# First of four weight sums by a load and an adding transfer instead of by VectorE

## The reference

```python
proj = hn @ w_in                       # hn: 512 x 2048
...
g = jax.nn.sigmoid(gate_logits.reshape(b, s, N_BRANCHES, D_MODEL))
y = g[:, :, 0] * ua + g[:, :, 1] * ub + g[:, :, 2] * uc
return x + y @ w_out
```

## Time and profile before

| | |
|---|---|
| median of 3 runs | 2146.58 us (2145.89 to 2147.29) |
| span of the profiled execution, first to last instruction | 2144.3 us |
| TensorE busy | 2114.5 us, 99% |
| VectorE busy | 1638.5 us, 76% |
| ScalarE busy | 920.1 us, 43% |
| GpSimd busy | 76.9 us, 4% |
| share of the chain that ended last: TensorE, VectorE, ScalarE, transfers | 83%, 6%, 3%, 2% |
| mean granted TensorE clock | 1.000 of full |

### The profile page before, as it was taken

How to read it: one execution, slowest core, us unless ns; L and a number is a source line. 1 busy time by engine, 2 the same in 40 slices (tenths; PEclk the granted TensorE clock), 3 DMA queues, 4 the chain that set the end, 5 groups by cost and what they waited for, 6 DMA issues and landing times.

```text
span 2144.3 us, 35680 instructions
## 1 busy us (share of the span) xinstructions
PE 2114.5 (99%) x12168; PEld 1835.5 (86%) x12168; DVE 1638.5 (76%) x2684; ACT 920.1 (43%) x1581; POOL 76.9 (4%) x145
## 2 busy tenths in 40 slices
PE   7899999999999999999999999999999999999999
PEld 6788888788887999999998888888787888888999
DVE  6887877775667888888886666666868776777887
ACT  6434454433335444444444444444545444223433
POOL 0000000000000000000000000000000000010000
PEclk9999999999999999999999999999999999999999
DMA  9766432565544343343333222222222223665543
GB/s 381 266 243 234 178 96 97 208 219 191 177 144 132 123 144 128 121 142 131 119 105 119 89 88 88 88 90 87 70 81 78 89 89 121 205 213 181 193 142 109
DMA packets 85935, 310.76 MB, mean 145 GB/s; under 512 B 9765, under 2 KB 12213, under 8 KB 77505
## 3 DMA queue, kind: packets, MB, share of 16 engines
q1 hardware_dynamic: 71568, 258.24, 35.6%
q0 software_dynamic: 11520, 46.68, 6.2%
q10 hardware_dynamic: 2738, 4.47, 0.6%
HBM read 284.41 MB, written 24.94 MB: 144 GB/s over the span
## 4 chain that ended last, share of the span: by engine, by line
PE 83%; DVE 6%; ACT 3%; DVEq 3%; DMA 2%; issue 1%; ACTq 0%
PE bank L425 18%; PE bank L427 18%; PE bank L426 18%; PE bank L1172 9%; PE bank L1174 9%; PE bank L1173 9%; DVE w_lo L419 2%; ACT w_hi L409 1%; PE bank L554 1%; PE bank L585 1%; DMA w_raw<-stream 1%; DMA front_raw<-stream 1%; PE bank L567 1%; DVEq L414 1%; ACT probs L637 1%
## 5 line engine op out<-in xcount | busy, mean ns | idle before, releaser
L425 PE MATMUL bank<-x_hi,w_hi 128*128 128x512 f32 x2000 | 789.1, 395 | 3.6 <-ACTq L1357 1.2
L427 PE MATMUL bank<-x_hi,w_lo 128*128 128x512 f32 x2000 | 779.1, 390 | 0.0
L426 PE MATMUL bank<-x_lo,w_hi 128*128 128x512 f32 x2000 | 778.6, 389 | 0.0
L419 DVE TENSOR_TENSOR w_lo<-w_raw,w_hi 128x512 fp32r<-128x512 f32 x468 | 324.2, 693 | 315.6 <-ACT w_hi L409 286.6
L409 ACT ACTIVATE w_hi<-w_raw 128x512 fp32r<-128x512 f32 x468 | 295.9, 632 | 572.4 <-PE bank L427 477.0
L425 PEld LDWEIGHTS bank<-x_hi,w_hi 128*128 128x128 f32 x2000 | 375.4, 188 | 94.4 <-issue 8.9
L1172 PE MATMUL bank<-x_hi,pw_hi 128*128 128x256 f32 x1568 | 444.0, 283 | 0.8 <-issue 0.7
L1173 PE MATMUL bank<-x_lo,pw_hi 128*128 128x256 f32 x1568 | 443.7, 283 | 0.0
L1174 PE MATMUL bank<-x_hi,pw_lo 128*128 128x256 f32 x1568 | 443.7, 283 | 0.0
L427 PEld LDWEIGHTS bank<-x_hi,w_lo 128*128 128x128 f32 x2000 | 375.4, 188 | 79.6
L426 PEld LDWEIGHTS bank<-x_lo,w_hi 128*128 128x128 f32 x2000 | 375.7, 188 | 75.4 <-issue 0.2
(11 more groups left out here) (214 smaller groups left out, 1840.5 us busy)
## 6 DMA issues: line engine op xcount, KB each, us to landing
w_raw<-stream SPq DMA_DIRECT2D x234, 512.0 KB, 3.7
pw_raw<-stream SPq DMA_DIRECT2D x112, 512.0 KB, 4.6
wmod<-w_mod_rows SPq DMA_DIRECT2D x32, 1024.0 KB, 6.7
front_raw<-stream SPq DMA_DIRECT2D x16, 1024.0 KB, 9.0
wmod<-w_mod_rows POOLq DMA_DIRECT2D x16, 1024.0 KB, 5.2
sig_store<-logits POOLq DMA_DIRECT2D x45, 256.0 KB, 2.5
sig_back<-sig_store SPq DMA_DIRECT2D x8, 768.0 KB, 5.9
gate_sig<-sig_store SPq DMA_DIRECT2D x7, 768.0 KB, 5.8
```

The lines of the kernel that those rows point to most:

```text
L419: nc.vector.tensor_tensor(w_lo[:, q, :], raw_quarter(s), w_hi[:, q, :].bitcast(F32), ALU.subtract).then_inc(lo_ready, 1)
L425: nc.tensor.matmul(bank_ap[:, :tokens], hi, x_hi[:, kx, :], start=start, stop=False)
L426: nc.tensor.matmul(bank_ap[:, :tokens], hi, x_lo[:, kx, :], start=False, stop=False)
L427: return nc.tensor.matmul(bank_ap[:, :tokens], lo, x_hi[:, kx, :], start=False, stop=stop)
```

## The change

SyncE now loads a21 a second time, straight into `w_sum[0]` (`first_row_load`), and when that has landed GpSimd's queue issues a transfer of a22 from DRAM that adds to what lies there (`second_row_add`, `accum_op=ALU.add`). `first_sum_added` counts these, and it is what ScalarE's split of S1 and VectorE's S2 wait for. VectorE makes only S2, S3 and S4, so `w_sum_made` counts three for each pair. The load may only start when `w_sum[0]` is free: when the low part of S3 of the pair before is made (`pw_lo_ready`), or, for the first pair of a stage, when all the low parts of the input sums are (`t_ready` at 8 or 16). Two semaphores are saved elsewhere (`dist_loaded`, `urow_zeroed`).

```diff
+            def first_row_load(pair):
+
+                if pair.positive() and not (pair.i is None and pair.c == PAIRS):
+                    sp.wait_ge(pw_lo_ready, ((pair - 1).times(7) + 5).value())
+                else:
+                    sp.wait_ge(t_ready, pair.c // PAIRS * KT // 2 + KT // 2)
+                src = stream[(pair.times(2) + (PANELS + 1)).pick(), :, :8 * P]
+                sp.dma_start(w_sum[0][:, :], src.rearrange("a p n -> p (a n)")).then_inc(first_row_loaded, 16)
+
             def load_factor(l, i=None):
...
                 elif a == 0:
-                    sp.wait_ge(w_sum_made, ((pair - 2).times(4) + 4).value())
+                    sp.wait_ge(w_sum_made, ((pair - 2).times(3) + 3).value())
...
             for l in range(12):
                 load_factor(l)
+                if l == 5:
+                    first_row_load(At(0))
+                if l > 4 and l % 4 == 3:
+                    first_row_load(At(l // 4))
             with steps(sp, 1, PAIRS // 3) as i:
                 for l in range(12):
                     load_factor(l, i)
+                    if l % 4 == 3:
+                        first_row_load(At(l // 4, 3, i))
...
             for l in range(6):
                 load_factor(first + l)
+            first_row_load(At(PAIRS))
             sp.wait_ge(xp_stored, 16 * (KT - 2))
             for p in range(OUT_PAIRS):
                 back_load(2 + 2 * p)
                 for l in range(4 * p + 6, min(4 * p + 8, 4 * OUT_PAIRS)):
                     load_factor(first + l)
+                if p + 1 < OUT_PAIRS:
+                    first_row_load(At(PAIRS + p + 1))
...
-            act.wait_ge(urow_zeroed, 1)
+            act.wait_ge(shift_ready, 1)
...
-                    act.wait_ge(w_sum_made, (f.pair.times(4) + (f.o - 1)).value())
+                    if f.o == 2:
+                        act.wait_ge(first_sum_added, (f.pair + 1).times(16).value())
+                    else:
+                        act.wait_ge(w_sum_made, (f.pair.times(3) + (f.o - 2)).value())
...
-            mod_biases(KT, 4, 0.0).then_inc(shift_ready, 1)
             nc.vector.memset(urow[:, :PAD], 0.0)
             nc.vector.memset(urow[:, PAD + T:], 0.0)
-            dve.drain().then_inc(urow_zeroed, 1)
+            mod_biases(KT, 4, 0.0).then_inc(shift_ready, 1)
...
                 dve.drain()
-                if f.o == 2:
-                    for a in (2, 3):
-                        dve.wait_ge(raw_of(f, a)[1], raw_of(f, a)[2])
-                to, one, two, op = {2: (w_sum[0], a21, a22, ALU.add), 3: (w_sum[1], w_sum[0], a11, ALU.subtract),
+                if f.o == 3:
+                    dve.wait_ge(first_sum_added, (f.pair + 1).times(16).value())
+                if f.o == 5:
+                    dve.wait_ge(raw_of(f, 2)[1], raw_of(f, 2)[2])
+                to, one, two, op = {3: (w_sum[1], w_sum[0], a11, ALU.subtract),
...
-                if f.o in (0, 1, 2, 6) and f.ahead(3):
+                if f.o in (0, 1, 2):
                     weight_sum(f.ahead(3))
...
                 if s == 15:
-                    weight_sum(Factor(2))
                     factor_lo(Factor(1))
...
                     token_sums_lo(KT - 2)
-                    weight_sum(Factor(PRODUCTS + 2))
                     factor_lo(Factor(PRODUCTS + 1))
...
-            for b in range(3):
+            def second_row_add(pair):
+
+                pool.wait_ge(first_row_loaded, (pair + 1).times(16).value())
+                src = stream[(pair.times(2) + (PANELS + 1)).pick(), :, 8 * P:].rearrange("a p n -> p (a n)")
+                pool.dma_start(w_sum[0][:, :], src, accum_op=ALU.add).then_inc(first_sum_added, 16)
+
+            for b in range(2):
                 sigmoid_store(At(b), At(1), b, b % 2)
+            second_row_add(At(0))
+            sigmoid_store(At(2), At(1), 2, 0)
+            second_row_add(At(1))
...
+                sigmoid_store(At(3 + 2 * b, 6, i) if i else At(3 + 2 * b + 6 * n), At(2, 2, i) if i else At(2 + 2 * n), b, 0)
+                if i:
+                    second_row_add(At(b + 2, 3, i))
+                elif 3 * n + b + 2 < PAIRS:
+                    second_row_add(At(3 * n + b + 2))
+                sigmoid_store(At(4 + 2 * b, 6, i) if i else At(4 + 2 * b + 6 * n), At(3, 2, i) if i else At(3 + 2 * n), b, 1)
...
             pool.dma_start(x_store[KT - 1, :, :], x_prime[:, :]).then_inc(xp_stored, 16)
+            for p in range(OUT_PAIRS):
+                second_row_add(At(PAIRS + p))
```

More of the change, by code:

```diff
@@ L314, in program @@
         mem_loaded = [sem(f"mem_part{n}_loaded") for n in range(4)]
-        c_loaded, dist_loaded = sem("c_loaded"), sem("dist_loaded")
+        c_loaded = sem("c_loaded")
         x_loaded = [sem(f"x_part{n}_loaded") for n in range(4)]
@@ L336, in program @@
         mem_k_ready, mem_v_ready, mem_out_stored = sem("mem_k_ready"), sem("mem_v_ready"), [sem(f"mem_out{n}_stored") for n in range(2)]
-        urow_zeroed, urow_ready, urow_used = sem("urow_zeroed"), sem("urow_ready"), sem("urow_used")
+        urow_ready, urow_used = sem("urow_ready"), sem("urow_used")
         sig_ready, sig_used = sem("sig_ready"), sem("sig_used")
@@ L348, in program @@
         pw_loaded = [sem(f"pw_raw{n}_loaded") for n in range(6)]
+        first_row_loaded, first_sum_added = sem("first_row_of_sum_loaded"), sem("first_sum_added")
         w_sum_made, pw_hi_ready, pw_lo_ready = sem("w_sum_made"), sem("pw_hi_ready"), sem("pw_lo_ready")
@@ L775, in dve_window @@
                 if s == 1 and w.extra:
-                    dve.wait_ge(dist_loaded, 16)
+                    dve.wait_ge(cols_loaded, 32)
                     dve.wait_ge(c_stored, 16)
@@ L986, in load_factor @@
                 elif a == 2:
-                    sp.wait_ge(w_sum_made, ((pair - 1).times(4) + 4).value())
+                    sp.wait_ge(w_sum_made, ((pair - 1).times(3) + 3).value())
                 else:
-                    sp.wait_ge(w_sum_made, ((pair - 1).times(4) + 3).value())
+                    sp.wait_ge(w_sum_made, ((pair - 1).times(3) + 2).value())
                 src = stream[(pair.times(2) + (PANELS + a // 2)).pick(), :, a % 2 * 8 * P:(a % 2 + 1) * 8 * P]
@@ L1550, in _ @@
                 split_hi(act, At(4 * FIRST["b"] - 3 + t))
-            act.dma_start(dist_a[:, :], dist_in).then_inc(dist_loaded, 16)
+            act.dma_start(dist_a[:, :], dist_in).then_inc(cols_loaded, 16)
             for _ in range(COPIES - 1):
@@ L1967, in weight_sum @@
             def weight_sum(f):
-                a11, a12, a21, a22 = (raw_of(f, a)[0] for a in range(4))
+                a11, a12, a21 = (raw_of(f, a)[0] for a in range(3))
                 dve.drain()
-                if f.o == 2:
-                    for a in (2, 3):
-                        dve.wait_ge(raw_of(f, a)[1], raw_of(f, a)[2])
-                to, one, two, op = {2: (w_sum[0], a21, a22, ALU.add), 3: (w_sum[1], w_sum[0], a11, ALU.subtract),
+                if f.o == 3:
[3 more added lines that the diff above has]
+                to, one, two, op = {3: (w_sum[1], w_sum[0], a11, ALU.subtract),
                                     4: (w_sum[0], a12, w_sum[1], ALU.subtract), 5: (w_sum[1], a11, a21, ALU.subtract)}[f.o]
@@ L2298, in sigmoid_store, with pair_sigmoids @@
                                logits[slot][:, :]).then_inc(sig_stored[slot], 16)
-            for b in range(3):
+            def second_row_add(pair):
[3 more added lines that the diff above has]
+            for b in range(2):
                 sigmoid_store(At(b), At(1), b, b % 2)
+            second_row_add(At(0))
+            sigmoid_store(At(2), At(1), 2, 0)
+            second_row_add(At(1))
             pool.wait_ge(c_neg_ready, 1)
             pool.dma_start(c_store, f_a[:HEADS_B, :]).then_inc(c_stored, 16)
-            with steps(pool, 0, PAIRS // 3) as i:
+            def pair_sigmoids(b, i, n):
+                sigmoid_store(At(3 + 2 * b, 6, i) if i else At(3 + 2 * b + 6 * n), At(2, 2, i) if i else At(2 + 2 * n), b, 0)
[4 more added lines that the diff above has]
+                sigmoid_store(At(4 + 2 * b, 6, i) if i else At(4 + 2 * b + 6 * n), At(3, 2, i) if i else At(3 + 2 * n), b, 1)
+            with steps(pool, 0, PAIRS // 3 - 1) as i:
                 for b in range(3):
-                    for e in range(2):
-                        sigmoid_store(At(3 + 2 * b + e, 6, i), At(2 + e, 2, i), b, e)
+                    pair_sigmoids(b, i, None)
+            for b in range(3):
+                pair_sigmoids(b, None, PAIRS // 3 - 1)
             pool.wait_ge(c_stored, 16)
```

## The result

The changed kernel takes 2199.93 us (median of 4 runs, 2197.9 to 2202.19), the kernel before, beside it, 2146.23 us (2145.43 to 2147.29). The ratio is 1.025, with a 95% interval of 1.0235 to 1.0266: 2.5% slower, some 54 us, where 12.3 were forecast. The profiled execution has a span of 2196.3 us, 52.0 above that of before.

The account below looks back on a forecast made before the run. TensorE was taken as the bound; 2.5 + 8.3 + 1.5 = 12.3 us on the span of 2144.3 gave 2156.6 in a profile, 2158.9 us as the runs' median. Own range 2154.8 to 2160.6, 8-in-10 range 2153 to 2200.

Parts of the forecast that it names:

- What bounds the kernel: TensorE bounds it; VectorE's work in the pairs is hidden behind matmuls, so removing sums buys nothing inside a stage.
- The start of the first stage: TensorE's product 2 of the first paired stage waits for S1, at 711.1 instead of 708.6: loss 2.5 us.
- The start of the second stage: TensorE's product 2 waits for load and adding transfer, at 2013.7 instead of 2005.44: loss 8.3 us.
- The clock: Behind the second stage's first wait, matmuls run at half speed for a while: 1.5 us, bounds 0 and 2.2.
- The loop: In steady pairs, buffer free, load, add, split and VectorE's chain take 14.5 us + A, within a pair's 20.2.
- A: Time from GpSimd's issue to the landing of a22 added into w_sum[0]: taken as 5.2 us.
- the forecast's limit: In the steady pairs, the adding transfer may take at most 5.7 us for the turn to fit 20.2 us.
- the forecast's formula: In each later pair, TensorE waits for A - 5.7 us if A is over 5.7 us.
- The load's own term: In the steady pairs, the load of a21, third of a burst, takes 6.0 us.
- The first: Rival: A over 5.7 us, so TensorE waits in each of 26 later pairs; 2196 us at A = 7.0; chance 0.35.
- The second (not slower): Rival: the first S1 of each stage comes in time; gain up to 1.3 us, 2145.3 us; chance 0.05.
- The third: Rival: the clock does not fall, 2157.4 us, or the second start's load takes 6.5 us, 2161.5; no separate chance.

Follow-up runs that it names:

- the kernel with held blocks: Changed kernel with the load ahead of the pair's two blocks, and those blocks held until the adding transfer has landed: 2158.17 us.
- the copy: Changed kernel with GpSimd's transfer copying a22 over w_sum[0] instead of adding it: 2171.53 us; also with the load issued before the two blocks: 2178.93 us.
- the load ahead: Changed kernel with SyncE issuing the load of a21 into w_sum[0] before the pair's two blocks, not behind them: 2205.59 us.
- the kernel with S1's own buffer: Changed kernel with a separate buffer for S1, its load issued before the two blocks once S1's low part is made: 2162.74 us.

## Why the prediction was right or wrong

**What bounds the kernel: right.** VectorE's sums lie beside matmuls. With the loop closed and the starts given back, 26 of 28 sums gone leave 2147.42 us against 2146.48.

**The start of the first stage: right.** Forecast were the issue at 703.1, product 2 at 711.1 and a loss of 2.5 us. It was issued at 702.62, and TensorE's row is

```profile
710.62 0.39 PE L1191 MATMUL bank<-x_hi,pw_hi 128*128 128x256 f32 x1 [1.96 <-DVE pw_lo L1985]
```

a loss of 2.0 against the 708.6 of before. The transfer took 5.4 us.

**The start of the second stage: right.** Everything there is some 29 us later than before. The load took 4.0 us (3.9 forecast), the adding transfer 5.7, by GpSimd's and VectorE's rows:

```profile
2034.45 0.90 POOL L2323 DMA_DIRECT2D w_sum<-stream  x1 [29.59 <-DMA w_sum<-stream]
```

```profile
2040.22 1.23 DVE L1998 TENSOR_TENSOR w_sum<-w_sum,pw_raw 128x1024 f32<-128x1024 f32 x1 [10.05 <-DMA w_sum<-stream]
```

and TensorE's wait is 9.4 us, as forecast:

```profile
2033.17 0.28 PE L1193 MATMUL bank<-x_hi,pw_lo 128*128 128x256 f32 x1
2042.86 0.55 PE L1191 MATMUL bank<-x_hi,pw_hi 128*128 128x256 f32 x1 [9.42 <-issue]
```

Product 0 had begun at 2027.53, so product 2 came 15.3 us after it, and 7.0 before (1998.44 to 2005.44): a loss of 8.3, the forecast's number.

**The clock: too small for this kernel.** The forecast held 1.5 us, with bounds of 0 and 2.2, all behind the second start's wait. In the changed kernel half-speed matmuls cost 2.8 us there (0.21 us apart from 2042.86 to 2048.97, at a granted clock of 0.50), and 1.6 more behind the first start's wait (from 710.62 to 714.33, at 0.55), where none were forecast. That is 4.4 us, 3.9 more than before. In the kernel with held blocks, with nearly the same two waits (2.07 and 9.1 us), it is 2.1 us, 1.6 more than before: there the forecast's number came out, in part by luck. The length of the rest alone does not tell whether half speed follows. After 2.92 us of rest the matmuls from 840.95 on are 0.21 us apart, and so they are after 1.96 us at 710.62; in the kernel with held blocks, after 2.07 us, they are 0.12 apart again from the second on, and the granted clock is 1.00 from 710 to 714. The Trainium skill's "TensorE: Matmul & The Clock Gate" (part 1) has as a rule that the throttled state is the default and activity releases it. The traces agree with the second half of it: full speed comes back while matmuls run, at 714.33, 844.10 and 2048.97. In the whole changed kernel the half-speed matmuls cost 10.8 us more than before, but by the sum below most of that is no extra: in a pair whose turn is set by the loop, slower matmuls only use up time in which TensorE would have waited. No run here tries this apart.

**The loop: the frame was right, and its size A failed.** The text reads "Sum: 14.5 + A. It must be at most 20.2, so A at most 5.7." The failed step is "I take 5.2, the row with as many bytes read, since writes can go beside reads", used for the steady pairs: there the transfer took 6.9 us in the first paired stage and 8.2 in the second. The limit was a little too high as well. In the changed kernel all but the adding transfer comes to 14.75 us in the first stage and 14.7 in the second, which leaves 5.4 to 5.5 for A; the copy took the 5.7 of the forecast's limit, and its loop did not close. With the medians the forecast's formula gives 1.2 us in 20 pairs and 2.5 in 6, 39 us; with the 12.0 by which the span of the kernel with held blocks, where only the starts are left, is over that of before, it is 51, against the 52.0 measured. With the table's mean turns in place of the formula it would be 55, so a hit within a microsecond is in part luck.

The load's own term was right (6.0 forecast, 5.7 measured), though a row was misread for it: the 6.5 us of the earlier trace rows belong to the second load of that burst, issued at 811.88. The third, issued at 813.33, took 6.3.

**Why A was off.** At the starts, with no block load beside it, it is 5.4 and 5.7 us, 0.2 to 0.5 above the row that I took. The rest is the block loads in flight beside it: 5.6 us in the median with none (the kernel with held blocks), 6.9 with two (19 of the 21 transfers of the changed kernel's first stage) and 8.6 with four (the load ahead). The forecast had a load's time in a burst (6.5 against 3.9) and used it for the load, but priced the adding transfer, which goes beside the same blocks, by the median of a row, without asking what stood beside that row's transfers. The sixteen of 1024 KB in the earlier trace rows were not alone either, and not alike: ten took 5.0 to 5.4 us, with one or two block loads beside them for a part of that time, and the six others 5.7 to 9.2. That spread was the warning. The mean share of 0.38 of the engines' time, which I held against the rival, says nothing of the moment in which the transfers meet: from 811 to 823 us the share was 0.58 in the kernel before, and from 800 to 815 us it is 0.82 in the changed one. So the forecast had a margin of 0.5 us a pair on a term with an error of over one, and a chance of 0.58 on the wrong side of it.

The estimate by the Trainium skill's "Collectives: The Full Stack" (bandwidth ceiling: a reduction costs two source reads, not the add) and "DMA: Bandwidth & Descriptors" (anatomy of a transfer) was 4.4 us. The trace does not agree: it is 5.4 to 5.7 with no block load beside it. A copy of as many KB took 3.8 to 4.2 at the same places, and the addition made it 1.2 to 1.9 longer.

**The rivals.** The first is what happened. Its 2196 us are 4 below the runs: its pairs (26 times 1.3, 34 us) are 5 below the 39 of the medians, its starts (15.9) are 4 above the 12.0, and the rest is the microsecond that is missing above and the profiled run, which was 2 us below the runs' median. The second (not slower) has nothing for it: the first S1 was late at both starts. The third puts both its times into the forecast's own range, but 2161.5 lies above that range's 2160.6. **VectorE's busy time** went down by 35 us (34 forecast), and the store behind the adding transfer went out late without anything waiting for it for more than 3.4 us in total.

What stays open: how much of the 8.2 us of the second stage comes from x1's loads and the results' stores, which only that stage has. With the blocks held the transfer took 5.5 us there, with the results' stores beside it; x1's loads stand behind the blocks in SyncE's queue and were held with them. In the last pair of the stage no block load is beside it, but x1's loads and the results' stores are: it took 7.2 us in the changed kernel (at 2168.63) and 5.7 where VectorE makes the first S1. So they can cost something without any block, and not always.

## What to carry to other kernels

Work taken off an engine that is not the bound buys nothing, but the transfers that replace it form a loop with the buffer they fill, and its length, not their bandwidth, has to stay under the period. Price each transfer of such a loop in the company that it will have there, beside the burst that is released at the same moment, and not by the median of a row of its kind; look at that row's single transfers and at what stood beside them. A margin of 0.5 us on a sum of 20 is no margin. Two ways closed the loop here: a buffer that comes free earlier, or holding back the transfers that nobody waits for until the one that is waited for has landed; and at the start of a stage, where nothing runs ahead, the old engine is best kept.

## What the runs showed of the hardware

- GpSimd's adding transfer of 512 KB took 5.4 to 5.7 us with no block load beside it, 6.9 in the median with two 512 KB loads in flight beside it (8.2 in the second stage, with x1's loads and the results' stores besides) and, in the medians, 8.6 to 9.1 with four; the plain copy took 3.8 to 4.2, 5.7 and 7.7. GpSimd is busy 0.90 us with issuing the one and 0.54 with the other.
- A 256 KB store issued 1 us behind an adding transfer on the same queue lands in 4.9 to 5.4 us even with no block load beside it (the kernel with held blocks), and in 6.9 in the median in the changed kernel, instead of 2.5. In the kernel with S1's own buffer, the stores issued 12 to 13 us behind one take 2.3 again; those 6 to 7 us behind, with block loads still landing, take 2.6 to 5.1.
- SyncE's load for S1 took 3.7 us in the median where no block load was issued with it, 4.2 to 4.4 where it was the first of a burst, and 5.7 to 6.3 where it was the third.
- TensorE's matmuls ran at half speed for some 3 us behind several rests of only 2 to 3 us (half-speed spacing from 840.95 to 844.10), yet not behind each: after 2.07 us of rest in the kernel with held blocks they were 0.12 apart from the second on, after 1.96 us in the changed kernel 0.21.
